# Up sums of the second half of the rows written two token quarters further on, so that the four products of a call use four column groups

## The reference

```python
def peer_layer(h, w_query, sub_keys, expert_down, expert_up):
    ...  # experts: (t, 8, 16) indices, gates: softmax of their scores
    def block(args):
        xb, eb, gb = args
        u = expert_down[eb]
        act = jax.nn.gelu(jnp.einsum('td,thkd->thk', xb, u), approximate=False) * gb
        vv = expert_up[eb]
        return jnp.einsum('thk,thkd->td', act, vv)
...
        x = x + gt2 * peer_layer(h2, w_query[l], sub_keys[l], expert_down[l], expert_up[l])
    return rms_norm(x, g_final)
```

## Time and profile before

| | us |
|---|---|
| median of 3 runs | 2970.42 (2962.66 to 2971.54) |
| profiled execution | 2969.21 |
| its span | 2967.4 |
| PE busy | 2264.3 (76%) |
| DVE busy | 1420.9 (48%) |
| ACT busy | 758.9 (26%) |
| POOL busy | 591.3 (20%) |
| L2595, products on ring buffers | 604.1, 1568 records |

### The profile page before, as it was taken

How to read it: one execution, slowest core, us unless ns; L and a number is a source line. 1 busy time by engine, 2 the same in 40 slices (tenths; PEclk the granted TensorE clock), 3 DMA queues, 4 the chain that set the end, 5 groups by cost and what they waited for, 6 DMA issues and landing times. The chain is left out here.

```text
span 2967.4 us, 28984 instructions
## 1 busy us (share of the span) xinstructions
PE 2264.3 (76%) x9828; PEld 967.2 (33%) x9828; DVE 1420.9 (48%) x3332; ACT 758.9 (26%) x1753; POOL 591.3 (20%) x587
## 2 busy tenths in 40 slices
PE   5997899987777775799988978867755655565554
PEld 2543444532222222755655443322211111111110
DVE  2575411410000001301377667667678777777765
ACT  3104301110000001312177653222222222222212
POOL 0000000010000001000112223344344433443442
PEclk9999999989998997799998889888777777778786
DMA  9168429589999996512447868899999999999996
GB/s 340 60 240 291 167 79 211 206 318 400 404 402 399 398 399 245 182 57 84 147 175 288 307 262 320 359 411 416 417 421 422 421 421 421 421 404 421 421 421 253
DMA packets 213260, 922.17 MB, mean 311 GB/s; under 512 B 18986, under 2 KB 58968, under 8 KB 121230
## 3 DMA queue, kind: packets, MB, share of 16 engines
q0 software_dynamic: 78864, 552.72, 45.9%
q1 hardware_dynamic: 124480, 359.15, 33.0%
q10 hardware_dynamic: 9790, 8.73, 0.9%
HBM read 888.78 MB, written 31.77 MB: 310 GB/s over the span
## 5 line engine op out<-in xcount | busy, mean ns | idle before, releaser
L2595 PE MATMUL bank<-ring,arena_w 128*32 128x512 f32 x1568 | 604.1, 790 | 310.8 <-ACT arena_w L1318 310.6
L885 POOL DMA_INDIRECT ring<-in_expert_pair,ids x392 | 414.9, 1058 | 1048.6 <-PE bank L2595 680.1
L1969 PE MATMUL bank<-arena_h,ring 128*128 128x128 f32 (+2 forms) x1264 | 363.3, 448 | 10.3 <-DMA ring<-in_w_in 7.9
L2249 PE MATMUL bank<-ring,arena_h 128*64 128x512 f32 x1056 | 271.1, 672 | 88.0 <-DMA ring<-in_w_exp_up 83.2
L2595 PEld LDWEIGHTS bank<-ring,arena_w 128*32 128x32 f32 x1568 | 104.6, 128 | 657.6 <-ACT arena_w L1318 467.4
L1918 DVE CUSTOM_DVE_ANT_0 ring<-ring,arena_h 128x1024 f32<-128x1024 f32 x203 | 244.9, 1225 | 80.4 <-DMA ring<-in_expert_pair,ids 48.6
L1918 DVE CUSTOM_DVE_ANT_0 ring<-ring 128x1024 f32<-128x1024 f32 x189 | 229.6, 1224 | 79.7 <-DMA ring<-in_expert_pair,ids 71.3
L1969 PEld LDWEIGHTS bank<-arena_h,ring 128*128 128x128 f32 x1264 | 204.1, 196 | 160.3 <-issue 127.3
L1316 ACT ACTIVATE arena_w<-arena_w 128x2 f32<-128x2 f32 x256 | 51.8, 202 | 769.7 <-DVE arena_w L1918 769.3
L1641 DVE TENSOR_TENSOR arena_q<-arena_q,bank 128x256 f32<-128x256 f32 x32 | 13.5, 421 | 484.3 <-ACT arena_q L1060 484.3
L2249 PEld LDWEIGHTS bank<-ring,arena_h 128*64 128x64 f32 x1056 | 91.9, 155 | 264.9 <-issue 259.5
(11 more groups left out here) (472 smaller groups left out, 3040.8 us busy)
## 6 DMA issues: line engine op xcount, KB each, us to landing
ring<-in_w_exp_gate SPq DMA_DIRECT2D x33, 2048.0 KB, 19.4
ring<-in_w_exp_up SPq DMA_DIRECT2D x33, 2048.0 KB, 23.8
ring<-in_w_exp_down SPq DMA_DIRECT2D x33, 2048.0 KB, 24.9
ring<-in_w_in SPq DMA_DIRECT2D x15, 2048.0 KB, 20.2
ring<-in_w_mod SPq DMA_DIRECT2D x12, 2048.0 KB, 19.3
ring<-in_w_ada SPq DMA_DIRECT2D x12, 2048.0 KB, 14.7
xs_d<-zeros SPq DMA_DIRECT2D x1, 12032.0 KB, 70.8
ys_d<-arena_h ACTq DMA_DIRECT2D x64, 128.0 KB, 7.3
```

The lines of the kernel that those rows point to most:

```text
L885: pool.indirect_dma_start(pair[pair_of(m)], None, A["expert_pair_2"], bass.IndirectOffsetOnAxis(ap=ids[n % 2][:, r:r + 1], axis=0)).then_i ...
L1969: mm = pe.matmul(dst, w[:, c, at], rhs[:, c, :], start=(c == 0), stop=(c == chunks - 1))
L2249: mm = pe.matmul(bank[2 + b][at, :].rearrange("p (g f) -> p g f", g=2), xbT[b][:, c, :], gu[:, :, c, 256 * half:256 * half + 256], start=( ...
L2595: mm = pe.matmul(bank[4 + 2 * (n // H % 2) + half][at, :], sel_q[:, n % 2, k0 + j, :], pair[pair_of(m + j)][:, D + 512 * half:D + 512 * ha ...
```

## The change

In half 1 a group's product is written two quarters further on (modulo four): groups 0 and 1 of a call then use column groups 0 and 1 in half 0, and 2 and 3 in half 1, or the other way round. So in banks 5 and 7 the tokens' rows 0 to 63 and 64 to 127 have changed places. `last_norm` puts them back: for the second half of the columns the product with `gt2_2` is made in two pieces of 64 partitions, each reading one half of the bank and writing the other half of `tmp_p`.

```diff
                 for j in range(2):
                     at = slice(512 * j, 512 * j + 512)
                     dve.wait_ge(peer_done, t + 1)
-                    link(dve.tensor_tensor(tmp_p, bank[4 + 2 * (t % 2) + j][:, :], gt2_2[:, at], ALU.mult))
+                    sums = bank[4 + 2 * (t % 2) + j]
+                    if j == 0:
+                        link(dve.tensor_tensor(tmp_p, sums[:, :], gt2_2[:, at], ALU.mult))
+                    else:
+
+                        for to, there in ((slice(0, 64), slice(64, P)), (slice(64, P), slice(0, 64))):
+                            link(dve.tensor_tensor(tmp_p[to, :], sums[there, :], gt2_2[there, at], ALU.mult))
                     link(dve.tensor_tensor(xr[:, t, at], xr[:, t, at], tmp_p, ALU.add), fin_add if j == 1 else None)
...
                 for half in range(2):
                     for j in range(count):
-                        at = slice(Q * ((k0 + j) % 4), Q * ((k0 + j) % 4) + Q)
+                        g = (k0 + j + 2 * half) % 4
+                        at = slice(Q * g, Q * g + Q)
                         mm = pe.matmul(bank[4 + 2 * (n // H % 2) + half][at, :], sel_q[:, n % 2, k0 + j, :],
                                        pair[pair_of(m + j)][:, D + 512 * half:D + 512 * half + 512], start=False, stop=False)
```

## The result

The changed kernel took 2996.99 us (median of 7) where the kernel before took 2974.64: ratio 1.0086, interval 1.0065 to 1.0107. The forecast of 2947.6 us was wrong in sign; what happened is rival (4), the one on TensorE's clock.

A forecast was written before the change was run, and what follows sets the result against it. PE's in-order queue was taken to bound the kernel from 1500 to 1880 us, the expert gathers afterwards. 5 + 14 + 6 + 0.8 - 3 = 22.8 us; 2969.2 - 22.8 + 1.2 = 2947.6 us, range 2924 to 2966.

The forecast's parts named there:

- rival (4): PE's granted clock from 1500 to 1880 us falls; below 0.776 the change loses, at 0.75 it takes 2982 us; chance 0.06.
- One call: One call of up_sums goes from four rounds of two to two rounds of four: 1.91 to 1.05 us, 45% saved.
- rival (3): Products within a call start in program order, not side by side; only the VectorE pieces remain, +0.7 us, 2971 us; chance 0.05.
- 1880 us and later worth nothing: From 1880 to 2950 us the gathers set the pace and their queue is full, so PE's savings give 0.
- 1500 to 1600 us, 5 us: Stick-breaking attention: of 9.7 us of PE time saved, 5 us arrive, bounds 0 and 9.7; DVE becomes fullest.
- rival (2): Sums only covered hand-overs; PE waits elsewhere, only 5 us of the chain and 0.8 of the tail arrive: 2965 us; chance 0.16.
- 1600 to 1745 us, 14 us won with bounds 3 to 20.8: Mostly forgetting attention, PE leading: two thirds of 20.8 us saved arrive, 14 us, bounds 3 and 20.8.
- 1745 to 1880 us, 6 us: 13 us of PE time could go; following the chain of the work that ended last, 6 us arrive, bounds 3 and 13.
- The tail, 0.8 us won: At the end of the span the last call saves about 1.5 us, the split closing costs 0.72; net 0.8 us won.
- The clock, 3 us lost: From 1500 to 1880 us, gaps opening where the sums were may lower PE's granted clock; 3 us taken off.

The follow-up runs named there:

- later_tiles_only: The changed kernel with the rotation and its split closings for tiles 1 to 3 (units 8 to 31) alone, tile 0 as before: 0.9991 of the kernel before.
- changed_again: The changed kernel, unaltered, measured once more beside other kernels on one chip: 1.0062 (1.0032 to 1.0091) of the kernel before.
- half_left_out: The kernel before with the products of half 1 left out in units 2 and 3, so part of the computation is missing: 1.0116 of the kernel before.
- one_product_filled: The changed kernel with one product of zeros added behind each call in units 2 and 3, in one column group: 1.0004 of the kernel before.

## Why the prediction was wrong, point by point

**One call**: right. 1.05 us was forecast, 1.06 measured, and the line's busy time on ring buffers fell from 604 to 409 us, 32%; four groups with four different moving operands run side by side, and rival (3), the strict order, fell. That makes the first half of what the prediction rested on sound; the error lies in what the saving does.

**1880 us and later worth nothing**: right, shown by later_tiles_only (0.9991).

**1500 to 1600 us, 5 us**: too high. Units 0 and 1 went from 146 to 144 us, their TensorE busy time from 132.0 to 123.1: 9 us less work gave 1 to 2 us. That is near the nothing that rival (2) gave this stage; what TensorE waits for instead was not followed up.

**1600 to 1745 us, 14 us won with bounds 3 to 20.8**: this is the stage where it failed. Units 2 and 3 took 32 us more in the execution shown and 17 in changed_again's. I had looked for what TensorE would wait for, and bounded the term by a yield between little and full. The bound below should have been negative: TensorE is busy nearly all the time there, and its products take longer at a lower clock (the score products 548 ns at a mean clock of 0.88, 819 at 0.61).

**1745 to 1880 us, 6 us**: units 4 to 7 won 4, about right as a number. Their TensorE busy time fell by 22 us, so there too most of the saving did not arrive; the clock fell from 0.84 to 0.78. (The prediction's own pieces of the chain add up to 6.1 + 0.9 = 7.0 us, where it took 6 and rival (2) 5; nothing hangs on that.)

**The tail, 0.8 us won**: 0. The terms were right (1.4 us won on the last call, 0.72 lost on the closing), but the zero products behind the call took 3.06 us instead of 2.21 and ate the rest.

**The clock, 3 us lost**: the step that failed. This term was mis-sized, and it carried the sign. The prediction let the clock fall only in gaps that open where the sums were; it stayed low while TensorE was busy. As an estimate, taking work at half the clock as twice as long, half of the low time is lost: in units 2 and 3 that is half of 129 us less half of 30, 49 us, and in changed_again (92 us low) 31 us, against the 3 taken off. With 49 us lost to the clock and 32 on balance, some 17 us of the saving did arrive; with 31 and 17, 14 us. By this estimate the 14 us forecast for this stage were not the error.

The four stages of the earlier trace rows after the change:

```profile
1500.00:1600.00 100.00, 84.88 (x516) 60.62 (x516) 79.54 (x185) 79.32 (x140) 23.24 (x20) 0.86 0.51 192
1600.00:1745.00 145.00, 133.61 (x552) 72.30 (x551) 83.47 (x213) 85.70 (x161) 33.96 (x32) 0.67 0.70 266
1745.00:1810.00 65.00, 49.01 (x208) 27.69 (x207) 36.45 (x78) 27.10 (x51) 11.74 (x12) 0.59 0.63 245
1810.00:1880.00 70.00, 59.99 (x237) 25.39 (x237) 52.86 (x123) 23.84 (x54) 21.32 (x20) 0.90 0.73 283
```

By their lengths the mean clock over 1500 to 1880 us is 0.75, under the 0.776 from which rival (4) said the change would lose. At 0.75 it gave 2982 us, 12 over before; measured were 17 to 22 over. The rest may be the full saving that it assumed and that did not arrive in units 0 and 1 and 4 to 7. I gave it 0.06 for two reasons. One was the stretch 1624 to 1645 us, 0.69 with TensorE busy throughout. I read it as "falls are no matter of gaps alone", which is right, and took it as evidence for the change. It was the warning. In this stretch the clock was low three times, at 1623, 1630 and 1640 us; the second fall came among the attention's products, without idle time, and the clock was back at 1626.5, 1636.75 and 1643.75 us, within 1.1 us of the end of a call of the sums each time. The rounds that the change would halve were what ran when the clock came back. The other, that the array does the same products in less time, was an argument without a row.

The Trainium skill ("TensorE: Matmul & The Clock Gate", "Part 1: The HAM clock gate (the "warmup" mystery)") ties the full clock to activity. By its advice against idle gaps, taken by itself, unit 3 of the changed kernel, busy 90.86 of 92 us at 0.57, should have stayed at the full clock; the rows show that it didn't. Nothing here tells what the hardware counts.

## What to carry to other kernels

Where TensorE is the bound and its granted clock is below 1, ask of every product that is made shorter or more parallel what then stands around it, and put a loss of the whole stretch at the lower clock into the lower bound; a row with a busy engine and a low clock marks such a place. Packing four column groups instead of two took a call from 1.91 to 1.06 us and made the whole slower; no run here shows a place where it pays. Compare the granted clock of each stage before and after, and not the span's mean: the fall from 0.79 to 0.58 over 940 us, where the DMA share is 1.01, cost nothing here, the one from 0.88 to 0.61 in units 2 and 3 cost more than the change could win. And look at how long each low stretch lasts, not only at how often the clock falls: it fell less often in the slower kernel.

## What the hardware showed that was not expected

Less work at TensorE made the kernel slower (half_left_out, 1.0116), and more work made the changed one faster (one_product_filled, 1.0004 against 1.0062 on the same chip). By the whole time, one empty product in a single column group did what four in all groups did (1.0004 and 1.0027, intervals that overlap); in unit 2 it did less. A product ran ahead of others that stand before it in the program when its column group was free (L2600 at 1699.17 us, before the second half of its call at 1700.02 us). A product over the whole array between two that use column groups, a single column wide, cost 0.43 us at the full clock. The VectorE product from PSUM took as long on 64 partitions, with the result moved by 64, as on 128 (1.41 us for two, 0.69 for one).
